# Expert weights read as one run per partition, with the tokens' features regrouped by a stride of 8

## The chip, the cores and the metric

The kernel runs on one core of a Trainium2 chip. The metric is the device time of one execution in microseconds (us). Less is better.

## What is computed

A network of three blocks on 512 tokens with 1024 features, in fp32. The change touches the first block's mixture of experts. Each token is sent to the best two of eight experts in the best of four groups (32 experts in all). Each expert has a gate and an up matrix of 1024 x 512 and a down matrix of 512 x 1024:

```python
def expert_block(args):
    xb, e = args
    a = xb @ w_e_gate[e]
    u = xb @ w_e_up[e]
    return (jax.nn.silu(a) * u) @ w_e_down[e]
...
y = jax.ops.segment_sum(y_rows * row_w[:, None], row_tok, num_segments=T)
```

The rows `xb` are tokens after an RMS norm whose gain vector `norm_ffn_g` has one factor per feature. Ahead of it come a gated convolution and a forgetting attention, behind it an mLSTM block with pooling and a latent attention block.

## The kernel before

The program is written engine by engine; semaphores order the engines against each other. Nothing schedules it: each engine's order is the order of the code.

**Dense products.** A weight matrix comes in slices of 256 columns, 1 MB each, through a ring of three buffers (`w_raw`). `load_slice(n)` on SP (L483 to L494) waits until the products of slice n - 3 are done and issues the load. ACT makes a high part of the slice (`w_hi`, L681), DVE the rest (`w_lo`, L1453), and PE multiplies in three passes (L1037 to L1039). Slices follow each other in the program's order: convolution (`cc`, `cu`, `cb`), `gconv`, `forget`, `conv_out`, then the attention's. ACT splits `conv_out`'s first slice after it has evicted the last `gconv` result.

**Experts.** Every expert gets a block of 64 token slots (`CAP`). Gate, up and down matrices have two buffers each, for even and odd experts. Experts 0 and 1 are loaded ahead (L497 to L499); the loop on SP (L524 to L532) loads expert e + 2's gate matrix when expert e's gate product is done, then up after the up product, and down after the down product. All three put 128 rows of the matrix on the 128 partitions: row `c * 128 + p` lies on partition p in chunk c, with 8 chunks for gate and up:

```python
gate_src = lambda e: t["w_e_gate"][bass.ds(e, 1)].rearrange("e (c p) n -> p (e c) n", p=P)
```

A partition thus reads 8 runs of 512 numbers (2 KB) for gate and for up, and 4 runs of 4 KB for down.

GpSimd gathers an expert's 64 rows of the normalised tokens from `h2_dram` into `xg` (64 partitions x 1024 features). On PE, `turn_rows` (L1205 to L1208) turns them so that features lie on the partitions: 8 transposes, each of which loads 128 columns of `xg` into the array and streams a 64 x 64 identity through it. DVE's `rows_in` (L1724) evicts the 8 results from PSUM to `xT` (128 x 8 x 64) and multiplies by the gain, of which `vec` holds feature `c * 128 + p` at partition p, column c. `xT` is the moving operand of the gate and up products, and its chunk c must hold the same features as chunk c of the matrix.

One expert on PE: gate product and up product, 64 matmuls each (fp32, 64 columns, L1215), then the turn of the **next** expert's rows, then the down product, 24 matmuls in three passes (L1037 to L1039). Beside it ACT and DVE split the down matrix (L681, L1741) and evict the results of the up product (L1748 to L1754).

```python
up_product(bank[2 + p], ring_gate[p], xT[p], gate_made)
...
up_product(bank[4 + p], ring_up[p], xT[p], up_made, bank[p], up_half)
...
turn_rows(1 - p, xt_turned)
```

The first turn stands ahead of the loop, so there are 33. Names used below: `xg` are the gathered rows, `xT` the turned ones, `down_hi` and `down_lo` the split down matrix, `hx` the product of silu(gate) and up, `gr` a small table loaded later in the program.

Of the kernel before, what the change touches and what calls it, by code (L numbers as in the profile page):

```python
# [16 lines left out]
F32 = mybir.dt.float32  # L17
# [7 lines left out]
P = 128  # L25
SEQ = 512
D = 1024
TT = SEQ // P
KC = D // P
# [8 lines left out]
CAP = 64  # L38
# [26 lines left out]
VECS = ["norm_mix_g", "conv_w0", "conv_w1", "conv_w2", "conv_b", "norm_ffn_g", "a_norm_g", "a_conv_w0",  # L65
        "a_conv_w1", "a_conv_w2", "a_conv_w3", "a_conv_b", "a_head_norm_g", "a_skip", "a_pool_scale", "c_norm_g"]
# [73 lines left out]
def build_kernel(nc, t):  # L140

    with ExitStack() as ctx:
        def at(name, shape, dt, offset):
            return nc.alloc_sbuf_tensor_at(name, shape, dt, offset=offset)
# [6 lines left out]
        def sem(name):  # L151
            if name not in sems:
                sems[name] = ctx.enter_context(nc.semaphore(name))
            return sems[name]


        bank = [ctx.enter_context(nc.psum_tensor(f"bank{i}", [P, 512], F32)) for i in range(8)]
# [6 lines left out]
        def misc(name, shape, dt):  # L164
            size = int(np.prod(shape[1:])) * (2 if dt == BF16 else 4)
            x = at(name, shape, dt, place[0])
            place[0] += -(-size // 32) * 32
            return x

        const = misc("const", [P, C_END], F32)  # L170
        vec = misc("vec", [P, V_END], F32)
# [22 lines left out]
        pos_i = misc("pos_i", [P, TT], I32)  # L194
        pos_f = misc("pos_f", [P, TT], F32)
        mark = misc("mark", [P, 8], F32)
        T0 = place[0]
        assert T0 + 12 * 2048 <= 229344, T0 + 12 * 2048

        def temp(name, i, shape=(P, 512), dt=F32, extra=0):  # L200
            return at(name, list(shape), dt, T0 + i * 2048 + extra)

        ident = const[:, C_ID:C_UP]
# [39 lines left out]
        xg = [at(f"xg{p}", [CAP, D], F32, BASE + 20480 + 4096 * p) for p in range(2)]  # L243
# [91 lines left out]
        x3_dram = nc.dram_tensor("x3_dram", (SEQ, D), F32).ap()  # L335
        h2_dram = nc.dram_tensor("h2_dram", (SEQ, D), F32).ap()
        y_dram = nc.dram_tensor("y_dram", (TOPK * SEQ + CAP, D), F32).ap()
        tok_view = lambda a: a.rearrange("(t p) d -> p t d", p=P)
        x_v = tok_view(t["x"])
        out_v = tok_view(t["out"])  # L340
# [3 lines left out]
        slice_no = {}  # L344
# [91 lines left out]
        def until_taken(eng, key):  # L436

            eng.wait_ge(drained[order[key] % 8], order[key] // 8 + 1)
# [45 lines left out]
        def _(sp):  # L484
# [13 lines left out]
                sp.dma_start(ring_up[p][:, :, :], up_src(e)).then_inc(up_landed[p], 16)  # L498
                sp.dma_start(ring_down[p][:, :, :], down_src(e)).then_inc(down_landed[p], 16)  # L499

            gate_src = lambda e: t["w_e_gate"][bass.ds(e, 1)].rearrange("e (c p) n -> p (e c) n", p=P)
            up_src = lambda e: t["w_e_up"][bass.ds(e, 1)].rearrange("e (c p) n -> p (e c) n", p=P)
            down_src = lambda e: t["w_e_down"][bass.ds(e, 1)].rearrange("e (c p) n -> p (e c) n", p=P)

            for tt in range(TT):
                sp.dma_start(x_tok[:, tt, :], x_v[:, tt, :]).then_inc(x_loaded[tt], 16)
            for n in range(slices1):
                if n == slice_no[("mix_out", 0)]:

                    until_taken(sp, ("OT1", KC - 1))  # L510
                    sp.dma_start(x1_tok[:, :, :], x_v).then_inc(x_back, 16)
                load_slice(n)
# [22 lines left out]
            with sp.If(count > 0):  # L535
                with sp.Fori(0, OVF) as i:
                    with sp.If(count > i):
                        sp.wait_ge(sem("ovf_free"), i + 1)
                        e = expert_of(i)
# [494 lines left out]
        def _(pe):  # L1034
# [156 lines left out]
            for b in range(TT):  # L1191
                ins = pe.matmul(out[:, TT * NE:(TT + 1) * NE], ones_b[:, :], hots[:, b, :, :].rearrange("p g e -> p (g e)"),
                                start=b == 0, stop=b == TT - 1)
# [4 lines left out]
            for q in range(TOPK * TT):  # L1198
                ins = pe.matmul(out[0:CAP, 0:NBLK], hot_slot[:, q, :], hot_block[:, q, :], start=q == 0, stop=q == TOPK * TT - 1)
# [4 lines left out]

            def turn_rows(p, done):  # L1205
                for j in range(KC):
                    ins = pe.transpose(bank[p][:, j * CAP:(j + 1) * CAP], xg[p][:, j * P:(j + 1) * P], ident[0:CAP, 0:CAP])
                ins.then_inc(done, 1)  # L1208

            def up_product(out, w, x, done, out2=None, half_done=None):  # L1210
# [19 lines left out]
            with pe.Fori(0, NE // 2) as i:  # L1230
                for p in range(2):
# [10 lines left out]
                    for f in range(FC):  # L1242
# [5 lines left out]
                        for a in range(2):  # L1248
                            half = slice(a * 512, (a + 1) * 512)
                            ins = parts3(bank[6 + a][:, :], hx_hi[p][:, f, :], hx_lo[p][:, f, :], down_hi[:, f, half],  # L1250
                                         down_lo[p][:, f, half], f == 0, f == FC - 1)
# [27 lines left out]
            for h in range(MH):  # L1279
                for tp in range(2):  # L1280
                    out = open_bank(pe, ("v2", h, tp))
                    for a in range(2):
                        tk = slice((2 * tp + a) * P, (2 * tp + a + 1) * P)
                        for c in (2 * h, 2 * h + 1):
                            ins = parts3(out[:, a * MD:(a + 1) * MD], xmT_hi[:, c, tk], xmT_lo[:, c, tk], wh[:, c, :], wl[:, c, :],
                                         c == 2 * h, c == 2 * h + 1)
# [3 lines left out]
            for name in ("q2", "k2"):  # L1290
                wh, wl = weights(slice_no[(name, 0)])
                for j in range(KC):
                    h, a = j // 2, j % 2
                    out = open_bank(pe, (name, j))
                    for c in (2 * h, 2 * h + 1):
                        ins = parts3(out[:, :], wh[:, c, a * P:(a + 1) * P], wl[:, c, a * P:(a + 1) * P], xcT_hi[:, c, :],
                                     xcT_lo[:, c, :], c == 2 * h, c == 2 * h + 1)
# [4 lines left out]
            for k, src in enumerate((g_i, g_e)):  # L1302
                for tt in range(TT):
                    ins = pe.transpose(out[:, (k * TT + tt) * MH:(k * TT + tt + 1) * MH], src[:, tt * P:(tt + 1) * P],
                                       ident[0:MH, 0:MH])
# [5 lines left out]
            for h in range(MH + 1):  # L1311
                if h < MH:
# [3 lines left out]
                    for sb in range(TT):  # L1316
                        out = open_bank(pe, ("ST", h, sb))
                        n = (TT - sb) * P
                        for c in (2 * h, 2 * h + 1):
                            ins = pe.matmul(out[:, 0:n], k2T[:, c, sb * P:(sb + 1) * P], q2T[:, c, sb * P:SEQ],  # L1320
                                            start=c == 2 * h, stop=c == 2 * h + 1)
                        ins.then_inc(results, 1)
                if h >= 1:
                    g = h - 1
                    for tt in range(TT):
# [5 lines left out]
                        for sb in range(tt + 1):  # L1331
# [3 lines left out]
                            ins = pe.matmul(out[:, MD:MD + 2], w, const[:, C_ONE:C_ONE + 2], start=False, stop=sb == tt,  # L1335
                                            skip_group_check=True)
# [12 lines left out]
            for j in range(KC):  # L1349
                g, a = j // 2, j % 2  # L1350
                out = open_bank(pe, ("pool", j))
                for c in (2 * g, 2 * g + 1):
                    ins = parts3(out[:, :], wh[:, c, a * P:(a + 1) * P], wl[:, c, a * P:(a + 1) * P], poolT_hi[:, c, :],
                                 poolT_lo[:, c, :], c == 2 * g, c == 2 * g + 1)
                ins.then_inc(results, 1)
            pe.wait_ge(sem("ya_lo_made"), KC)
            for c4 in range(4):
                banks = [open_bank(pe, ("w_out2", c4, tt)) for tt in range(TT)]
                for b, (xh, xl) in enumerate(((ya_hi, ya_lo), (yb_hi, yb_lo))):
# [3 lines left out]
                    for tt in range(TT):  # L1363
                        tk = slice(tt * P, (tt + 1) * P)
                        for c in range(KC):
                            ins = parts3(banks[tt][:, 0:256], xh[:, c, tk], xl[:, c, tk], wh[:, c, :], wl[:, c, :],
                                         b == 0 and c == 0, b == 1 and c == KC - 1)
# [30 lines left out]
            for s in range(4):  # L1398
                for name, c0, c1, n in (("uq", 0, nq, 2 * QKH), ("ukv", nq, 5, 512)):
                    wh, wl = weights(slice_no[(name, s)])  # L1400
                    for tt in range(TT):
                        out = open_bank(pe, (name, s, tt))
                        tk = slice(tt * P, (tt + 1) * P)
                        for c in range(c0, c1):
                            ins = parts3(out[:, 0:n], cT_hi[:, c, tk], cT_lo[:, c, tk], wh[:, c - c0, :], wl[:, c - c0, :],
                                         c == c0, c == c1 - 1)
# [31 lines left out]
        def _(dve):  # L1438
# [69 lines left out]
            for jj in range(4):  # L1508
                n = slice_no[("cc", jj)]
# [146 lines left out]
            for k, one in enumerate((one1, one2)):  # L1656
                ins = V.tensor_tensor(hot[:, k, :, :, :], one[:, :, :].unsqueeze(2).to_broadcast([P, TT, NG, EPG]),
                                      one_g[:, :, :].unsqueeze(3).to_broadcast([P, TT, NG, EPG]), ALU.mult)
# [59 lines left out]
            step(V.tensor_tensor(tok_w[:, 0, :], den, g_val, ALU.mult))  # L1718
            step(V.tensor_tensor(tok_w[:, 1, :], tok_w[:, 0, :], e2, ALU.mult))

            gain = vec[:, VECS.index("norm_ffn_g") * KC:(VECS.index("norm_ffn_g") + 1) * KC].unsqueeze(2).to_broadcast([P, KC, CAP])

            def rows_in(p, done):
                V.tensor_tensor(xT[p][:, :, :], bank[p][:, :].rearrange("p (c n) -> p c n", c=KC), gain, ALU.mult).then_inc(done, 1)  # L1724
# [11 lines left out]
            with dve.Fori(0, NE // 2) as i:  # L1736
                for p in range(2):
# [6 lines left out]
                    for half in range(2):  # L1744
                        n = FC // 2
# [46 lines left out]
            for s in range(4):  # L1792
                for j in (2 * s, 2 * s + 1):
# [8 lines left out]
                    for back in (1, 2, 3):  # L1802
                        ins = V.scalar_tensor_tensor(out=cv[:, back:], in0=src[:, 0:SEQ - back], scalar=vcol(f"a_conv_w{3 - back}", j),  # L1803
                                                     in1=cv[:, back:], op0=ALU.mult, op1=ALU.add)
# [34 lines left out]
            for h in range(MH + 1):  # L1839
                if h < MH:  # L1840
# [5 lines left out]
                    for sb in range(TT):  # L1846
# [5 lines left out]
                        n = (TT - sb) * P  # L1852
# [280 lines left out]
```

## Time and profile before

| | |
|---|---|
| runs shown | 2264.02, 2259.97, 2265.17 us |
| median | 2264.02 us |
| span of the profiled execution | 2262.5 us (its first to its last instruction) |
| PE busy | 2135.4 us, 94% of the span |
| DVE busy | 884.1 us, 39% |
| ACT busy | 709.5 us, 31% |
| moved by DMA | 335.00 MB, mean 148 GB/s |
| stage of the experts | about 791 to 1474 us of the span |

The profile is of one execution, and the page gives no time for it beside its span; what lies around the span, taken against the median, is 1.5 us. PE is TensorE's matmuls, PEld its loads of the stationary operand, DVE is VectorE, ACT ScalarE, POOL GpSimd, SP SyncE, which issues most DMAs. The granted clock (PEclk) is 1.00 at 2.4 GHz and 0.50 at 1.2 GHz. A line number such as L1207 is that of the kernel before.

### The profile page before, as it was taken

How to read it: one execution, taken by the hardware profiler on the slowest of the kernel's cores; microseconds unless marked ns; L12 is line 12 of the kernel's file. 1: busy time of each engine (PE TensorE's matmuls, PEld its weight loads, DVE VectorE, ACT ScalarE, POOL GpSimd, SP SyncE). 2: the span in 40 equal slices, each digit the busy share in tenths (PEclk: the TensorE clock that was granted, in tenths of full speed). 3: DMA queues.
4: the chain of work that ended last, by engine and by line, in shares of the span. 5: the costliest groups of instructions: out<-in, count | busy, mean ns of one | idle time of the engine just before them, and what ended most of it. 6: DMA issues, size and time to landing. Idle time of an engine off the chain costs nothing. (4 is left out here: it accounts for less than half of the span.)

```text
span 2262.5 us, 30876 instructions
## 1 busy us (share of the span) xinstructions
PE 2135.4 (94%) x12870; PEld 1862.6 (82%) x12870; DVE 884.1 (39%) x1476; ACT 709.5 (31%) x1010; POOL 103.3 (5%) x158
## 2 busy tenths in 40 slices
PE   7999999999999699999999999938999999998898
PEld 6888889766679599999999999836978889988568
DVE  4443221233344323323333333256343872335562
ACT  4222222322222303322332233243434222346431
POOL 0000000000000111110111011001000100000000
PEclk9999999755569779999999999969999999999899
DMA  6543555200015459999999999342312242222101
GB/s 140 94 98 98 96 96 96 68 1 0 1 50 190 173 181 335 334 330 330 332 334 328 331 332 334 130 181 84 94 38 75 75 132 94 71 76 69 47 1 56
DMA packets 189499, 335.00 MB, mean 148 GB/s; under 512 B 5088, under 2 KB 98016, under 8 KB 189408
## 3 DMA queue, kind: packets, MB, share of 16 engines
q1 hardware_dynamic: 183536, 315.32, 44.8%
q0 software_dynamic: 5440, 17.83, 2.1%
q8 instruction: 66, 1.08, 0.2%
q10 hardware_dynamic: 432, 0.56, 0.1%
q14 instruction: 25, 0.20, 0.0%
HBM read 318.49 MB, written 15.20 MB: 147 GB/s over the span
## 5 line engine op out<-in xcount | busy, mean ns | idle before, releaser
L1453 DVE TENSOR_TENSOR w_lo<-w_raw,w_hi 128x2048 fp32r<-128x2048 f32 (+2 forms) x97 | 211.6, 2183 | 474.8 <-ACT w_hi L681 474.6
L1741 DVE TENSOR_TENSOR down_lo<-down,down_hi 128x4096 fp32r<-128x4096 f32 x32 | 141.6, 4425 | 319.7 <-ACT down_hi L681 319.7
L681 ACT ACTIVATE w_hi<-w_raw 128x2048 fp32r<-128x2048 f32 (+2 forms) x97 | 176.8, 1823 | 266.5 <-PE bank L1039 114.8
L1215 PEld LDWEIGHTS bank<-xT,gate 128*128 128x128 f32 x2048 | 240.0, 196 | 3.5 <-issue 1.1
L1215 PE MATMUL bank<-xT,up 128*128 128x64 f32 x2048 | 240.5, 280 | 0.0
L1215 PE MATMUL bank<-xT,gate 128*128 128x64 f32 x2048 | 238.7, 279 | 0.9 <-DVE xT L1724 0.9
L1215 PEld LDWEIGHTS bank<-xT,up 128*128 128x128 f32 x2048 | 237.8, 196 | 0.0
L1037 PE MATMUL bank<-h1T_hi,w_hi 128*128 128x512 f32 x456 | 177.5, 389 | 0.6 <-DVE h1T_lo L1460 0.6
L1038 PE MATMUL bank<-h1T_lo,w_hi 128*128 128x512 f32 x456 | 177.4, 389 | 0.0
L1039 PE MATMUL bank<-h1T_hi,w_lo 128*128 128x512 f32 x456 | 177.4, 389 | 0.0
L681 ACT ACTIVATE ys<-bank 64x512 f32<-64x512 f32 x64 | 34.3, 584 | 425.2 <-PE bank L1039 425.2
L681 ACT ACTIVATE down_hi<-down 128x4096 fp32r<-128x4096 f32 x32 | 115.6, 3612 | 0.2
L1037 PE MATMUL bank<-h2T_hi,w_hi 128*128 128x512 f32 x264 | 103.6, 392 | 3.3 <-DVE hy_t L1890 2.2
L1037 PE MATMUL bank<-down_hi,hx_hi 128*128 128x512 f32 x256 | 104.3, 407 | 0.0
L1038 PE MATMUL bank<-h2T_lo,w_hi 128*128 128x512 f32 x264 | 103.4, 392 | 0.0
L1039 PE MATMUL bank<-h2T_hi,w_lo 128*128 128x512 f32 x264 | 103.4, 392 | 0.0
L1037 PEld LDWEIGHTS bank<-h1T_hi,w_hi 128*128 128x128 f32 x456 | 85.6, 188 | 18.6 <-issue 0.7
L1039 PE MATMUL bank<-down_hi,hx_lo 128*128 128x512 f32 x256 | 100.6, 393 | 0.0
L1038 PE MATMUL bank<-down_lo,hx_hi 128*128 128x512 f32 x256 | 100.2, 391 | 0.0
L1039 PEld LDWEIGHTS bank<-h1T_hi,w_lo 128*128 128x128 f32 x456 | 85.6, 188 | 17.7
L1038 PEld LDWEIGHTS bank<-h1T_lo,w_hi 128*128 128x128 f32 x456 | 85.6, 188 | 17.7
L1120 PE MATMUL bank<-v,pT_t 128*128 128x64 f32 (+1 forms) x480 | 98.8, 361 | 0.8 <-DVE pT_t L1585 0.8
(443 smaller groups left out, 4006.5 us busy)
## 6 DMA issues: line engine op xcount, KB each, us to landing
gate<-in_w_e_gate SPq DMA_DIRECT2D x32, 2048.0 KB, 9.9
up<-in_w_e_up SPq DMA_DIRECT2D x32, 2048.0 KB, 9.1
down<-in_w_e_down SPq DMA_DIRECT2D x32, 2048.0 KB, 10.1
w_raw<-in_w_in SPq DMA_DIRECT2D x32, 1024.0 KB, 9.6
w_raw<-in_a_w_in SPq DMA_DIRECT2D x20, 1024.0 KB, 5.2
w_raw<-in_a_w_out SPq DMA_DIRECT2D x8, 1024.0 KB, 5.3
w_raw<-in_c_w_in SPq DMA_DIRECT2D x6, 1024.0 KB, 5.3
w_raw<-in_w_conv_out SPq DMA_DIRECT2D x4, 1024.0 KB, 5.1
```

The costliest lines, as they stand in the source:

```text
L681: return nc.scalar.activation(out, in_, ACT.Copy, scale=scale)
L1037: pe.matmul(out, sh, mh, start=start, stop=False)
L1038: pe.matmul(out, sh, ml, start=False, stop=False)
L1039: return pe.matmul(out, sl, mh, start=False, stop=stop)
L1120: ins = pe.matmul(out[:, 0:width], pT_buf[k % 2][:, b, :], v_of(k, b), start=b == 0, stop=b == k % TT)
L1215: ins = pe.matmul(to[:, g * CAP:(g + 1) * CAP], w[:, c, f * P:(f + 1) * P], x[:, c, :], start=c == 0, stop=c == KC - 1)
L1453: V.tensor_tensor(ring_view(w_lo, n), ring_view(raw, n), ring_view(w_hi, n).bitcast(F32), ALU.subtract)\
L1741: V.tensor_tensor(down_lo[p][:, :, :], ring_down[p][:, :, :], down_hi[:, :, :].bitcast(F32), ALU.subtract)\
```

## The change

Gate and up matrices are put on the partitions in another order: row `p * 8 + c` lies on partition p in chunk c, so that the 8 rows of a partition are one run of 16 KB in DRAM. The down matrix keeps its order. `turn_rows` takes every eighth feature of `xg`, beginning at j, for its transpose j, so that `xT` has the same order as the matrices. The gain must be in that order too: a new tile `gain_pc` (128 x 8) replaces the slice of `vec`. It is made once: SP copies the 1024 gains from the input `vecs` to a DRAM tensor in the order of the features, in pieces of 4 bytes, waits for it, and loads them with 8 neighbours on each partition. DVE waits for this (`gain_loaded`) ahead of the loop.

```diff
+        gain_pc = misc("gain_pc", [P, KC], F32)
...
+        gain_dram = nc.dram_tensor("gain_dram", (D, 1), F32).ap()
...
-            gate_src = lambda e: t["w_e_gate"][bass.ds(e, 1)].rearrange("e (c p) n -> p (e c) n", p=P)
-            up_src = lambda e: t["w_e_up"][bass.ds(e, 1)].rearrange("e (c p) n -> p (e c) n", p=P)
+            gate_src = lambda e: t["w_e_gate"][bass.ds(e, 1)].rearrange("e (p c) n -> p (e c) n", p=P)
+            up_src = lambda e: t["w_e_up"][bass.ds(e, 1)].rearrange("e (p c) n -> p (e c) n", p=P)
...
             for n in range(slices1):
+                if n == slice_no[("conv_out", 0)]:
+                    g0 = VECS.index("norm_ffn_g") * KC
+                    sp.dma_start(gain_dram.rearrange("(c p) o -> p c o", p=P), t["vecs"][:, g0:g0 + KC].unsqueeze(2),
+                                 allow_slow_non_contiguous=True).then_inc(sem("gain_loaded"), 16)
+                    sp.wait_ge(sem("gain_loaded"), 16)
+                    sp.dma_start(gain_pc[:, :], gain_dram.rearrange("(p c) o -> p (c o)", p=P)).then_inc(sem("gain_loaded"), 16)
...
             def turn_rows(p, done):
                 for j in range(KC):
-                    ins = pe.transpose(bank[p][:, j * CAP:(j + 1) * CAP], xg[p][:, j * P:(j + 1) * P], ident[0:CAP, 0:CAP])
+                    rows = xg[p][:, :].rearrange("t (p c) -> t c p", c=KC)
+                    ins = pe.transpose(bank[p][:, j * CAP:(j + 1) * CAP], rows[:, j, :], ident[0:CAP, 0:CAP])
                 ins.then_inc(done, 1)
...
-            gain = vec[:, VECS.index("norm_ffn_g") * KC:(VECS.index("norm_ffn_g") + 1) * KC].unsqueeze(2).to_broadcast([P, KC, CAP])
+            gain = gain_pc[:, :].unsqueeze(2).to_broadcast([P, KC, CAP])
+            dve.wait_ge(sem("gain_loaded"), 32)
```

Two places show what this does to the order of instructions. The first is SP's queue at the end of the convolution, where `w_raw` is the ring of weight slices. Before:

```order
L494 DMA w_raw_49<-in_w_in 128x8x256 [waits results]
L494 DMA w_raw_50<-in_w_forget 128x1024 [waits results]
L494 DMA w_raw_51<-in_w_conv_out 128x8x256 [waits results]
L494 DMA w_raw_49<-in_w_conv_out 128x8x256 [waits results]
L494 DMA w_raw_50<-in_w_conv_out 128x8x256 [waits results]
```

With the change:

```order
L496 DMA w_raw_49<-in_w_in 128x8x256 [waits results]
L496 DMA w_raw_50<-in_w_forget 128x1024 [waits results]
L512 DMA gain_dram<-in_vecs 128x8x1
L515 DMA gain_pc<-gain_dram 128x8 [waits gain_loaded]
L496 DMA w_raw_51<-in_w_conv_out 128x8x256 [waits results]
```

The two small transfers, with the wait between them, stand ahead of the first load of `w_conv_out`; nothing else of the queue has moved.

The second is DVE ahead of the loop over the experts, from its last step of the routing to the first eviction of turned rows. Before:

```order
L1719 TENSOR_TENSOR tok_w<-tok_w,sm 128x4 [waits dve_step]
L1732 MEMSET hx_hi_135 128x512 [waits results,dve_step]
L1733 MEMSET hx_lo_137 128x512
L1732 MEMSET hx_hi_136 128x512 [waits dve_step]
L1733 MEMSET hx_lo_138 128x512
L1724 TENSOR_TENSOR xT_144<-bank,vec 128x512 [waits xt_turned,dve_step]
```

With the change:

```order
L1728 TENSOR_TENSOR tok_w<-tok_w,sm 128x4 [waits dve_step]
L1742 MEMSET hx_hi_136 128x512 [waits results,gain_loaded,dve_step]
L1743 MEMSET hx_lo_138 128x512
L1742 MEMSET hx_hi_137 128x512 [waits dve_step]
L1743 MEMSET hx_lo_139 128x512
L1734 TENSOR_TENSOR xT_145<-bank,gain_pc 128x512 [waits xt_turned,dve_step]
```

The first memset now waits for the gain as well, and the eviction reads `gain_pc`; the count and the order of the instructions are the same.

## Rows read from the trace of the kernel before

**Rows 1.** The page, part 1: busy us (share of the span) xinstructions.

```profile
PE 2135.4 (94%) x12870; PEld 1862.6 (82%) x12870; DVE 884.1 (39%) x1476; ACT 709.5 (31%) x1010; POOL 103.3 (5%) x158
```

**Rows 2.** Busy time by stretch: us, each engine's busy us, PEclk, DMA share, GB/s.

```profile
850.00:1440.00 590.00, 590.00 (x4609) 558.54 (x4609) 191.24 (x229) 183.81 (x146) 64.21 (x116) 1.00 0.96 329
```

**Rows 3.** Timeline of one expert: start us, us, engine, line [idle before].

```profile
1204.10 4.42 DVE L1741 TENSOR_TENSOR down_lo<-down,down_hi 128x4096 fp32r<-128x4096 f32 x1 [9.61 <-ACT down_hi L681]
...
1206.59 0.37 SPq L528 DMA_DIRECT2D gate<-in_w_e_gate  x1
...
1219.71 7.25 PE L1215 MATMUL bank<-xT,gate 128*128 128x64 f32 x64
1219.90 0.37 SPq L532 DMA_DIRECT2D down<-in_w_e_down  x1
...
1226.80 7.31 PE L1215 MATMUL bank<-xT,up 128*128 128x64 f32 x64
1227.14 0.37 SPq L528 DMA_DIRECT2D gate<-in_w_e_gate  x1
...
1234.04 0.71 PE L1207 MATMUL bank<-const,xg 64*128 64x64 f32 x8
```

**Rows 4.** The page, part 6: DMA issues of the experts, median us to landing.

```profile
gate<-in_w_e_gate SPq DMA_DIRECT2D x32, 2048.0 KB, 9.9
...
down<-in_w_e_down SPq DMA_DIRECT2D x32, 2048.0 KB, 10.1
```

**Rows 5.** Busy time by stretch while e1 is loaded ahead.

```profile
756.00:768.00 12.00, 12.00 (x92) 12.00 (x92) 0.00 (x0) 4.81 (x7) 1.49 (x2) 0.83 1.04 401
```

**Rows 6.** Waits of PE from 780 to 1470 us: us in total, times, longest.

```profile
PE bank L1207 <- DMA xg<-h_dram,get_row: 6.4, 1, 6.4
```

**Rows 7.** Busy time by stretch: the gate product beside loads and without.

```profile
1199.70:1206.20 6.50, 6.50 (x60) 6.50 (x60) 2.10 (x1) 4.30 (x3) 2.21 (x4) 1.00 0.97 337
1445.90:1452.40 6.50, 6.50 (x60) 6.46 (x59) 1.50 (x1) 4.58 (x3) 2.21 (x4) 1.00 0.21 45
```

**Rows 8.** L1207: the turn's loads (ns min/median/max), and timelines at both clocks.

```profile
L1207 PEld LDWEIGHTS bank<-const,xg x8: 178/221/221, 791.5 to 792.2; 64*128 64x128 f32 x8
...
L1207 PEld LDWEIGHTS bank<-const,xg x8: 134/138/142, 1213.5 to 1213.9; 64*128 64x128 f32 x8
...
821.01 0.93 PEld L1207 LDWEIGHTS bank<-const,xg 64*128 64x128 f32 x8
822.05 0.29 PEld L1037 LDWEIGHTS bank<-down_hi,hx_hi 128*128 128x128 f32 x1
...
1213.47 0.57 PEld L1207 LDWEIGHTS bank<-const,xg 64*128 64x128 f32 x8
...
1214.11 0.19 PEld L1037 LDWEIGHTS bank<-down_hi,hx_hi 128*128 128x128 f32 x1
```

**Rows 9.** Groups on DVE from 771 to 792 us: count | busy, mean ns.

```profile
L1674 DVE TENSOR_REDUCE counts<-hot_slot 128x8 f32<-128x256 f32 x1 | 0.4, 420 | 0.0
...
L1648 DVE TENSOR_REDUCE les<-wide 128x32 f32<-128x128 f32 x1 | 0.4, 375 | 0.0
...
L1649 DVE TENSOR_REDUCE sm<-les 128x4 f32<-128x32 f32 x1 | 0.2, 186 | 0.0
```

**Rows 10.** DMA issues with small pieces and of w_conv_out, median us to landing.

```profile
w_raw<-in_w_conv_out SPq DMA_DIRECT2D x4, 1024.0 KB, 5.1
...
gr<-in_c_kn_rope_g SPq DMA_DIRECT2D x1, 32.0 KB, 9.9
```

**Rows 11.** Timelines of SP and of ACT around the first load of w_conv_out.

```profile
177.30 0.34 SPq L494 DMA_DIRECT2D w_raw<-in_w_forget  x1
188.18 27.57 SPq L494 DMA_DIRECT2D w_raw<-in_w_conv_out  x4
...
199.56 1.91 ACT L681 ACTIVATE w_hi<-w_raw 128x2048 fp32r<-128x2048 f32 x1
```

**Rows 12.** Timeline before the first turn: the first gather.

```profile
787.52 0.96 POOL L596 DMA_INDIRECT xg<-h_dram,get_row  x1 [0.28 <-POOL get_row L604]
```

## The prediction

> **What bounds the kernel now.** I began with the page's shares: PE is busy for 2135.4 of 2262.5 us, 94% of the span [rows 1]. The change touches the stage with the experts, so next I asked for busy time by stretch. From 850 to 1440 us PE is busy for all of 590 us at a granted clock of 1.00, while the DMA share stands at 0.96 with 329 GB/s [rows 2]. Two resources look full at once; the two views after that tell which of them is the bound.
>
> First, the rhythm of one expert in order of time. The gate loads are issued at 1206.59 and 1227.14, so an expert takes 20.55 us, and PE goes from the gate product (1219.71, 7.25 us) to the up product (1226.80) to turning the next rows (1234.04) without a gap [rows 3]. A gate load is issued when the gate product of the expert two before it ends. It lands a median 9.9 us later [rows 4], and its matrix is wanted 34 us after the issue (two periods less the 7.25 us product): some 24 us to spare. The up load has as much. The down load is issued at 1219.90 and lands 10.1 us later, at 1230.0; its first reader, ScalarE's split, waits for the next down product's end, near 1240.5: 10 us to spare.
>
> Second, DMA has room. While expert 1 is loaded ahead, with nothing else in flight, the engines move 401 GB/s [rows 5], against 329 in the loop; the stretch holds pieces of 2 KB (gate, up) and of 4 KB (down). A DMA share near 1 at 329 GB/s is therefore overlapping transfers waiting on one another, not a queue that PE waits for. The list of PE's waits between 780 and 1470 us has one entry on a DMA, 6.4 us for the first gather, ahead of the loop [rows 6]. And loads do not slow PE down either: the same 6.5 us of the gate product hold 60 matmuls with DMA at 337 GB/s and 60 with 45 GB/s [rows 7]. **PE alone sets the 20.55 us.**
>
> **The change, part by part.**
>
> *Loads of 16 KB.* 64 transfers of 2 MB keep their bytes, but each partition now reads one run of 16 KB where it read eight of 2 KB. Whatever that saves lies in the 24 us to spare: 0. The cover is PE's 20.55 us per expert. It is gone only if PE needs less than DMA at its best: 6.3 MB at 400 GB/s are 15.7 us an expert; from there each per cent of rate would be worth 0.16 us an expert, 5 us in all. A worse rate would not be seen soon either: DMA can lose nearly a fifth (from 400 to 329 GB/s) before PE waits. The issue on SP stays one instruction per load. Gathers share the engines with longer pieces now, but one that is issued in an expert's gate product is read at the end of the next expert's up product, over 20 us on, so a few us of delay are free too: 0.
>
> *The turn with stride 8.* This is the part on the path. `turn_rows` runs once ahead of the loop and 32 times in it, 8 transposes each, 264 in all; [rows 8] has two of the turns. The rows xg are the operand that is loaded into the array; each load still takes 128 elements, but 32 bytes apart instead of side by side. Eight loads took 0.57 us with a median of 0.138 us for one, so one follows the other every (0.57 - 0.138) / 7 = 0.062 us; from the first load to the first load of the down product it is 1214.11 - 1213.47 = 0.64 us [rows 8]. Nothing hides more of it: the down product follows at once, whose low halves are made by 1208.5 (1204.10 + 4.42) [rows 3], and hx's second half is wanted only after 12 of its 24 matmuls. So every ns that a load takes longer is added 8 times per turn, 33 times.
>
> The trace of before has no strided load on PE. Bounds: at the low end 0, the load still pipelined at 0.062 us. Below nothing I exclude, since 128 elements must be read as before. At the high end the slowest stream of fp32 columns through PE in this stage: the gate product's 64 matmuls take 1226.80 - 1219.71 = 7.09 us, 0.111 us for 64 columns, which for 128 is 0.222 us: (0.222 - 0.062) x 8 x 33 = +42 us. Between them stand two near rows. One is the same turn where the granted clock was 0.50 (1.2 GHz, not 2.4): 822.05 - 821.01 = 1.04 us instead of 0.64 [rows 8], what it takes when columns come at half speed: +0.40 us. The other is a read with just this step of 32 bytes, on DVE: the sum over groups at L1648 reads 128 elements 8 apart in 0.375 us. Contiguous sums of 32 and 256 elements took 0.186 and 0.420 us [rows 9], so 1.04 ns per element, and 128 of them would cost 0.286 us. So the step made reading dearer by 0.089 us over 128 elements, 1.74 ns for one instead of 1.04: 1.7 times. It is the only row with this step, and it says that SBUF reads at 32 bytes come at something like half rate. I take half rate for PE too: +0.40 us a turn, 33 x 0.40 = **+13.2 us**.
>
> The Trainium skill, SBUF — State Buffer, in the note on cachelines under "Door 1: The DMA port swizzle", speaks against this change: lines of SBUF are 16 bytes, full bandwidth wants at least two hits in a line, and fp32 may stride by less than four elements for free. A step of 8 gives one hit per line; the page has no price, so by it the sum is more than 0 and no more can be said. The DVE row agrees, and no row here shows it for PE.
>
> *The gain.* `gain_pc` replaces a slice of `vec` in the multiplication that evicts xT (same shape, broadcast the same way): 0. Its making adds two DMAs on SP between the load of `w_forget` (177.30) and that of the first `w_conv_out` (188.18) [rows 11], and a wait for the first of them: 1024 pieces of 4 bytes from DRAM to DRAM. Behind the waiting SP stands the load of `w_conv_out`. SP is free for 10.5 us there anyway, since it waits for a result of PE. The nearest row is a load with pieces of 256 bytes, gr: 9.9 us with other loads about it [rows 10], so SP is back by 187.6, before 188.18. And were it 6 us later: the load takes 5.1 us [rows 10], landing at 193.3, and its split starts at 199.56 [rows 11]. 16 us in all, hence 0; beyond them each us late is a us of PE. The wait for `gain_loaded` on DVE comes 600 us later: 0.
>
> **Sum:** 0 + 13.2 + 0, on a profiled span of 2262.5 us: 2275.7. The median of the runs shown, 2264.02, has 1.5 us more around it than the span. Predicted 2277 us.
>
> **Rivals.**
>
> *A. The step costs PE nothing (0.32).* For it: PE reads through other hardware than DVE, and at a clock of 0.50 a load came every (0.93 - 0.221) / 7 = 0.101 us, at 1.00 every 0.062, not half of that [rows 8], so some of it is not column time and could hide a slower read. Against it: the part that is column time is the larger, and little would be hidden. Then nothing on the path changes: 2264. The Trainium skill, TensorE: Matmul & The Clock Gate, "LDWEIGHTS (loading the stationary operand)", has a load cost its columns divided by 1.2, in ns, and nothing else: 107 ns before and after. The trace has 62 ns from load to load, so the figure fails here, though its silence about strides may hold.
>
> *B. Each element costs PE a fetch of its own at the rate of the dear stream, 0.222 us a load (0.12).* For it: PE's loads run faster than one element per 0.5 ns, much faster than DVE's 1.04, so the fall could be steeper. Against: a ratio of 3.6, twice DVE's. +42 us: 2306.
>
> *C. SP comes back late (0.03).* It decides if the 4-byte pieces need more than 16 us to land; at 24 us PE stands 8 us: with the forecast's turn 2285. Against it: the small transfer of rows 10 needs 9.9 us.
>
> *D. The loads do bind, at the stage's start (0.05): faster.* Expert 1's load and the store of h2 lie right before the first gather, for which PE waits 6.4 us [rows 6]; with quicker loads the store and gather would come sooner. It decides only if the gather waits for engines. Against: it is issued at 787.52, after the table of rows is made [rows 12], when expert 1 has long landed. It needs rival A beside it; price: at most the whole wait: 2264 - 6.4 = 2257.6.
>
> That the pieces don't grow (16 KB cut again on the way) changes no term; it would show in the packet count alone.
>
> **How the numbers follow.** Forecast 0.48, A 0.32, B 0.12, C 0.03, D 0.05. About 0.2% (4.5 us) can be told from no change here. Faster is D, 0.05; same is A, 0.32; slower is the forecast, B and C, 0.63. The likeliest case's own range is a rate 1.45 to 2.2 times slower, 90 to 136 ns a load, +7.4 to +19.5 us: 2271 to 2284. The range must take in A with the scatter of the runs (2260 to 2265), and above a load of up to 150 ns (+23 us): 2260 to 2288. It leaves out B, and most of D and C.
>
> **What would show it.** Right: the eight loads of a turn take about 0.9 to 1.0 us instead of 0.57, the period grows from 20.55 to 20.95 us, gate and up products keep their 7.25 and 7.31 us, PE stays without idle time, and packets under 8 KB fall by some 65,000. The gate and up loads land earlier and nobody is earlier for it. Wrong: 0.57 us again (A), over 1.5 us (B), a hole in PE near 204 us (C), a shorter wait at 791 us (D); or a DMA-bound loop, seen as PE idle before L1215.

## The result and the profile after

The changed kernel takes 2274.57 us (median of 5 runs, 2270.27 to 2275.38), the kernel before 2264.67 us (5 runs, 2259.97 to 2265.9): 9.9 us more, a ratio of 1.0042 with a 95% interval of 1.003 to 1.0055. The profiled execution took 2274.69 us, 1.9 us of it around its span of 2272.8; its span is 10.3 us longer than that of before.

The page, the busy shares and the packets, beside [rows 1]:

```profile
PE 2145.7 (94%) x12870; PEld 1873.5 (82%) x12870; DVE 887.0 (39%) x1476; ACT 709.7 (31%) x1010; POOL 103.4 (5%) x158
...
DMA packets 133340, 335.01 MB, mean 147 GB/s; under 512 B 6273, under 2 KB 99201, under 8 KB 125057
```

PE has as many instructions as before and is busy 10.3 us longer: the whole loss is work of PE, not waiting. The pieces did grow: before, 189,408 of 189,499 packets were under 8 KB, now there are 64,351 fewer of these. Of 8 KB or more there were 91 and are now 8283, 8192 more: one for each of 128 partitions in 64 transfers, so the 16 KB went whole.

Where PE's time went is seen in one turn. Timeline of PE's loads (start us, us, engine, line, operation), one turn at a granted clock of 1.00, then one at 0.50, beside [rows 8]:

```profile
1220.01 0.96 PEld L1216 LDWEIGHTS bank<-const,xg 64*128 64x128 f32 x8
1221.03 0.19 PEld L1045 LDWEIGHTS bank<-down_hi,hx_hi 128*128 128x128 f32 x1
...
821.04 0.96 PEld L1216 LDWEIGHTS bank<-const,xg 64*128 64x128 f32 x8
822.12 0.28 PEld L1045 LDWEIGHTS bank<-down_hi,hx_hi 128*128 128x128 f32 x1
```

And all loads of the turn together (ns min/median/max, first and last start):

```profile
L1216 PEld LDWEIGHTS bank<-const,xg x264: 182/202/205, 791.5 to 1471.9; 64*128 64x128 f32 x132
```

Eight loads take 0.96 us instead of 0.57, and the down product starts 1.02 us after the first load instead of 0.64: +0.38 us for each turn at full clock. One load follows the other every (0.96 - 0.202) / 7 = 0.108 us, before every 0.062. At the half clock the 0.96 us are the same, where the contiguous turn took 0.93 [rows 8], and the down product comes after 1.08 us instead of 1.04. The stride costs 0.04 us there.

The loop over the experts, by its loads of the down matrix on SP (count, ns min/median/max, first and last start). First the kernel before, then the changed one:

```profile
L532 SPq DMA_DIRECT2D down<-in_w_e_down x30: 372/373/373, 829.1 to 1425.6; - x30
```

```profile
L540 SPq DMA_DIRECT2D down<-in_w_e_down x30: 383/383/390, 829.2 to 1436.1; - x30
```

That is 29 periods of 20.57 us before and of 20.93 after: +0.36 us each and +10.4 us together, about the whole difference of the spans (10.3). Two more turns come after the last of these loads. By the row above, the last load of a turn starts at 1471.9 us; before it was this:

```profile
L1207 PEld LDWEIGHTS bank<-const,xg x264: 134/139/221, 791.5 to 1460.7; 64*128 64x128 f32 x132
```

The stage begins at the same time in both. So the turns cost 11.2 us in all, 0.36 for each of the 31 at full clock, and the rest of the program took 0.9 us less, for which no run shows a reason.

Inside a period nothing else has changed. The up and gate products of the changed kernel, beside [rows 3]:

```profile
1212.77 7.31 PE L1224 MATMUL bank<-xT,up 128*128 128x64 f32 x64
...
1226.61 7.25 PE L1224 MATMUL bank<-xT,gate 128*128 128x64 f32 x64
```

Landings (median us, last column) beside [rows 4], the loop's busy time beside [rows 2], and the burst in which expert 1 is loaded ahead beside [rows 5]:

```profile
gate<-in_w_e_gate SPq DMA_DIRECT2D x32, 2048.0 KB, 8.8
up<-in_w_e_up SPq DMA_DIRECT2D x32, 2048.0 KB, 7.8
down<-in_w_e_down SPq DMA_DIRECT2D x32, 2048.0 KB, 8.5
```

```profile
756.00:768.00 12.00, 12.00 (x92) 12.00 (x92) 0.00 (x0) 4.81 (x7) 1.49 (x2) 0.83 0.96 392
850.00:1450.00 600.00, 600.00 (x4609) 569.25 (x4607) 193.68 (x228) 184.08 (x146) 64.32 (x116) 1.00 0.88 323
```

The gate loads land 1.1 us and the down loads 1.6 us earlier, the DMA engines are busy for 0.88 of the loop instead of 0.96, and PE is as full as before. Nobody waits for a load, so nobody is earlier. PE's waits from 780 to 1480 us are the same three as before, with the same 6.4 us for the first gather, beside [rows 6]:

```profile
PE bank L1216 <- DMA xg<-h_dram,get_row: 6.4, 1, 6.4
```

SP at the end of the convolution, beside [rows 11]:

```profile
177.28 0.34 SPq L496 DMA_DIRECT2D w_raw<-in_w_forget  x1
177.67 0.70 SPq L512 DMA_DIRECT2D gain_dram<-in_vecs  x1
187.15 0.35 SPq L515 DMA_DIRECT2D gain_pc<-gain_dram  x1
188.16 27.57 SPq L496 DMA_DIRECT2D w_raw<-in_w_conv_out  x4
```

The 4-byte pieces landed 9.5 us after their issue. SP was through with its next issue at 187.50, 0.7 us before PE's result let it go on, and the load of `w_conv_out` starts when it did before.

### The profile page after: what moved, and what is told of

Read it like the earlier page. It is cut to its first block and busy times, and to the rows that moved or that the text cites. A ratio compares the mean times of both kernels' runs of the same rounds, so it can differ in the third digit from the quotient of the medians.

```text
span 2272.8 us, 30878 instructions
## 1 busy us (share of the span) xinstructions
PE 2145.7 (94%) x12870; PEld 1873.5 (82%) x12870; DVE 887.0 (39%) x1476; ACT 709.7 (31%) x1010; POOL 103.4 (5%) x158
## 3 DMA queue, kind: packets, MB, share of 16 engines
q8 instruction: 66, 1.08, 0.2%
```

## The experiments

Two theories stood at the start. The first is the forecast's: only the turn costs, and 16 KB are worth nothing here. The rival is that 16 KB gain something and the turn costs more than the 10 us seen. Two kernels each make one half of the change.

**The turn alone.** The kernel before with only this:

```diff
-                    ins = pe.transpose(bank[p][:, j * CAP:(j + 1) * CAP], xg[p][:, j * P:(j + 1) * P], ident[0:CAP, 0:CAP])
+                    rows = xg[p][:, :].rearrange("t (p c) -> t c p", c=KC)
+                    ins = pe.transpose(bank[p][:, j * CAP:(j + 1) * CAP], rows[:, j, :], ident[0:CAP, 0:CAP])
```

> The kernel before with the turn alone changed: transposes read every eighth feature, the matrices stay in pieces of 2 KB and the gain is as before. (The rows then don't match the matrices, so the experts compute something else of the same size.) Theory, the turn's loads pay for the step: a load follows the other every 0.108 us instead of 0.062, the period is 20.92 us and the time is that of the changed kernel, about 10 us over before (2274 to 2276). Rival, the long pieces or the way to the gain slow the loop: the period stays 20.56 and the time that of before.

Measured: 2272.32 us against 2262.86 for the kernel before beside it, 1.0043 (1.003 to 1.0057). The loads have a median of 202 ns, the period is 20.92 us. The turn by itself makes the whole of the change's ratio.

**The loads alone.** The changed kernel, with the grouping by 8 moved from PE's reads to ScalarE's copy that makes the rows. They are stored in the new order, and the turn is contiguous again:

```diff
-                copy(h2_tok[:, tt, :], x1_tok[:, tt, :], rstd[:, tt:tt + 1]).then_inc(sem("h2_rows"), 1)
+                copy(h2_tok[:, tt, :].rearrange("t (c p) -> t p c", p=P), x1_tok[:, tt, :].rearrange("t (p c) -> t p c", c=KC),
+                     rstd[:, tt:tt + 1]).then_inc(sem("h2_rows"), 1)
...
-                    rows = xg[p][:, :].rearrange("t (p c) -> t c p", c=KC)
-                    ins = pe.transpose(bank[p][:, j * CAP:(j + 1) * CAP], rows[:, j, :], ident[0:CAP, 0:CAP])
+                    ins = pe.transpose(bank[p][:, j * CAP:(j + 1) * CAP], xg[p][:, j * P:(j + 1) * P], ident[0:CAP, 0:CAP])
```

> The changed kernel with 16 KB pieces and the reordered gain, but ScalarE writes the normalised rows into h2_tok already in the order p, c, so that the turn reads 128 neighbours as before. The result is the reference's. Theory: loads back at 0.062 us, period 20.56, time that of before within 2 us, since nothing waits for the matrices. If the long pieces had a gain of their own on the path, it would come out below before; if they had a cost, at 2266 or more. The four strided copies on ScalarE may take longer, but lie in 8 us of spare time.

Measured: 2264.37 us (11 runs) against 2262.86, 1.0004 (0.9995 to 1.0013). Loads of the turn, and PE's first wait in the stage (us in total, times, longest):

```profile
L1216 PEld LDWEIGHTS bank<-const,xg x264: 133/139/222, 792.6 to 1462.9; 64*128 64x128 f32 x132
```

```profile
PE bank L1208 <- DVE hot_block L1704: 6.8, 1, 6.8
```

The loads are back at 139 ns and the period at 20.57 us, with the landings of the changed kernel (8.8, 7.8, 8.5 us). So pieces of 16 KB are worth nothing in the period of this kernel. The stage begins 1.1 us later (792.6 against 791.5), with a wait of 6.8 us instead of 5.4 ahead of it; ScalarE's four copies that write the rows took 2.00 us each instead of 1.14. By the interval, from 1.1 us less to 2.9 us more than before, and with that late start, a gain or loss of some 2 us outside the loop is not excluded.

**Which steps cost?** By the 16-byte lines of the Trainium skill that the prediction cited (SBUF — State Buffer, the note on cachelines), a step of 8 bytes (two hits in a line) should cost less than 32 bytes. If distance counts, 16 bytes should cost less too. Both kernels keep the changed kernel's structure with smaller groups `c`. They also shorten the pieces, to 8 KB and 4 KB; between 16 and 2 KB the experiment above shows no difference beyond its interval. The main lines of the first edit:

```diff
-            gate_src = lambda e: t["w_e_gate"][bass.ds(e, 1)].rearrange("e (p c) n -> p (e c) n", p=P)
+            gate_src = lambda e: t["w_e_gate"][bass.ds(e, 1)].rearrange("e (b p c) n -> p (e b) (c n)", p=P, c=4)
...
-                    rows = xg[p][:, :].rearrange("t (p c) -> t c p", c=KC)
-                    ins = pe.transpose(bank[p][:, j * CAP:(j + 1) * CAP], rows[:, j, :], ident[0:CAP, 0:CAP])
+                    rows = xg[p][:, :].rearrange("t (b p c) -> t b c p", p=P, c=4)
+                    ins = pe.transpose(bank[p][:, j * CAP:(j + 1) * CAP], rows[:, j // 4, j % 4, :], ident[0:CAP, 0:CAP])
```

> As the changed kernel, but with a step of 4 features (16 bytes) and pieces of 8 KB. Theory, what counts is how many 16-byte lines of SBUF a load opens: with a step of 4 it still opens one for each element, so a load costs the same 0.108 us and the time is that of the changed kernel (+10 us). Rival, the price grows with the distance: about half, 0.085 us and +5 us.

> As the changed kernel, but with a step of 2 features (8 bytes) and pieces of 4 KB. Theory, lines: two elements per line, loads at 0.062 us, time that of before. Rival, any step breaks the fast path: 0.108 us and +10 us. Rival, distance: a quarter of the price, 0.074 us and +3 us.

Measured: 2276.4 us (1.0062, 1.0047 to 1.0078) with 16 bytes, 2280.45 us (1.0071, 1.0056 to 1.0087) with 8. A turn in each, 16 bytes first:

```profile
1219.31 1.03 PEld L1216 LDWEIGHTS bank<-const,xg 64*128 64x128 f32 x8
1220.41 0.19 PEld L1045 LDWEIGHTS bank<-down_hi,hx_hi 128*128 128x128 f32 x1
```

```profile
1202.19 1.03 PEld L1216 LDWEIGHTS bank<-const,xg 64*128 64x128 f32 x8
1203.29 0.19 PEld L1045 LDWEIGHTS bank<-down_hi,hx_hi 128*128 128x128 f32 x1
```

The eight loads take 1.03 us in both, slightly more than with 32 bytes, and a typical period is 21.00 us. Both theories fall, and the third of the last expectation, that any step pays, stands: the full price is paid at the smallest step that isn't 1, with two numbers in a line or with one. Why 8 and 16 bytes cost 0.07 us a turn more than 32 is open. The pattern differs in more than the step there: the slices begin in two or four blocks. At the half clock too the down product comes later with them, after 1.15 us, where it was 1.04 contiguous and 1.08 with 32 bytes.

The second kernel's profiled execution has something else besides. Two of its periods take 22.6 us; these stretches of it (length, busy us of PE, PEld, DVE, ACT, POOL, then granted clock, DMA share, GB/s) show why:

```profile
1040.00:1050.00 10.00, 10.00 (x92) 10.00 (x91) 4.42 (x1) 4.48 (x4) 2.21 (x4) 1.00 0.93 315
1050.00:1060.00 10.00, 10.00 (x57) 8.77 (x57) 2.30 (x7) 0.00 (x0) 0.00 (x0) 0.83 0.92 347
...
1260.00:1270.00 10.00, 10.00 (x65) 9.08 (x64) 2.56 (x8) 0.00 (x0) 0.00 (x0) 0.83 0.90 329
```

The 0.83 are the mean of 10 us. In slices of 1 us the clock is 1.00 up to 1054, 0.50 from 1055 to 1058 and 1.00 again from 1059, while PE was busy all the time: 2 x 1.6 = 3.2 us that belong to no step. Only this execution was profiled, but every run has a mean clock on record, and the time follows it: 2282.7 and 2281.87 us at 0.915 and 0.914, 2279.03 at 0.916, and 2276.14 at 0.918, which is the time of the kernel with 16 bytes (2276.4). The intervals of the two kernels overlap, so no price of 8 bytes over 16 is shown.

**What are 16 KB worth with less work on PE?** Two kernels, the one before and the changed one, with this in the gate and up products:

```diff
-                    for c in range(KC):
+                    for c in range(2):
                         ins = pe.matmul(to[:, g * CAP:(g + 1) * CAP], w[:, c, f * P:(f + 1) * P], x[:, c, :],
-                                        start=c == 0, stop=c == KC - 1)
+                                        start=c == 0, stop=c == 1)
```

> The kernel before with the gate and up products cut to 2 of 8 chunks (16 matmuls instead of 64 each; the sums over the other 6 chunks are left out), all loads kept. PE then needs 20.56 - 2 x 48 x 0.111 = 9.9 us per expert, and the loads should bind: 6.3 MB and 0.5 MB of rows at 401 GB/s are 17.0 us. It is the kernel that the next one is compared with.

> The changed kernel, cut in the same way, against the run before it. This shows what pieces of 16 KB are worth once nothing hides them. Theory, they raise the rate a little: the median landing in the loop fell from 9.9 to 8.8 us for gate and from 9.1 to 7.8 for up, so some 0.5 to 1.3 us per expert, 15 to 40 us in all. Rival, the engines are as fast with 2 KB: while expert 1 is loaded ahead, DMA moved 401 GB/s before and 392 after, so no difference.

Measured: 2186.41 us with 2 KB and 2186.55 with 16 KB. The same, but the pair doesn't answer the question. The periods are 18.70 and 18.69 us, not the 17.0 expected, and PE waits for the half of hx that comes last (2 KB, then 16 KB):

```profile
PE bank L1037 <- DVE hx_lo L1754: 206.2, 31, 7.4
```

```profile
PE bank L1045 <- DVE hx_lo L1764: 194.3, 31, 7.0
```

Behind that stands a chain: the down product frees the buffer, ScalarE and VectorE split, the next down product of 24 matmuls follows, at a granted clock of 0.77 in this loop. So I shortened this link too. In a second pair the down product is one pass:

```diff
-                            ins = parts3(bank[6 + a][:, :], hx_hi[p][:, f, :], hx_lo[p][:, f, :], down_hi[:, f, half],
-                                         down_lo[p][:, f, half], f == 0, f == FC - 1)
+                            ins = pe.matmul(bank[6 + a][:, :], hx_hi[p][:, f, :], down_hi[:, f, half], start=f == 0, stop=f == FC - 1)
```

> The kernel before with its loop over the experts made short enough for the loads to bind: the gate and up products add up only 2 of their 8 chunks, and the down product is one pass of 8 matmuls instead of three of 24 (the sums are not the experts' any more; every load, gather, split and turn is kept). What is left per expert beside the loads is ScalarE's split (3.6 us), VectorE's (4.4 us) and a down product of some 3 to 5 us, one after the other: 11 to 13 us. 6.3 MB of weights and 0.5 MB of rows at 400 GB/s are 16 to 17 us. I expect a period of 16 to 17 us, some 370 to 400 GB/s in the loop, the down load waiting on SP for less than before, and a time of about 2186 - 2 x 31 = 2125 us (2105 to 2150). If instead the period stays near 18.7 us, something other than loads or the down chain held the earlier pair.

> The changed kernel with the same cuts. Theory 1, pieces of 16 KB are worth nothing in rate: the burst ahead of the stage moved 401 GB/s with pieces of 2 KB and 392 with 16 KB, so the period is within 0.2 us of the other's, and the time within 6 us of it. Theory 2, they are worth what the DMA share shows, 0.88 instead of 0.96 in the loop for 323 against 329 GB/s, some 6% of the engines' time per byte: a period shorter by 0.6 to 1.0 us, and a time lower by 20 to 30 us. The landings, shorter by 1.1 to 1.6 us in the changed kernel's own loop, speak for theory 2; the burst speaks for theory 1.

Measured: 2154.99 us (2153.33 to 2157.36) with 2 KB, 2130.42 us (2127.75 to 2132.27) with 16 KB: 24.6 us or 1.1% less with 16 KB, so theory 2. With 2 KB the level is higher than the 2105 to 2150 us expected, since the loop moves less than 400 GB/s. Stretch 850 to 1250 and the down loads' issues with 2 KB, then the same with 16 KB:

```profile
850.00:1250.00 400.00, 200.09 (x1059) 178.87 (x1058) 142.10 (x176) 138.59 (x110) 48.70 (x88) 0.64 1.04 376
...
L532 SPq DMA_DIRECT2D down<-in_w_e_down x30: 372/6467/8686, 803.8 to 1324.4; - x30
```

```profile
850.00:1250.00 400.00, 195.41 (x1140) 174.33 (x1140) 148.57 (x184) 148.60 (x118) 53.12 (x96) 0.70 1.01 398
...
L540 SPq DMA_DIRECT2D down<-in_w_e_down x30: 383/384/390, 803.6 to 1294.7; - x30
```

That the loads bind now is seen on ScalarE. Its split of the down matrix waits for the down load, 104.4 us in all with 2 KB and 76.2 with 16 KB:

```profile
L681 ACT ACTIVATE down_hi<-down 128x4096 fp32r<-128x4096 f32 x32 | 115.7, 3616 | 104.4 <-DMA down<-in_w_e_down 104.4
```

```profile
L689 ACT ACTIVATE down_hi<-down 128x4096 fp32r<-128x4096 f32 x32 | 115.7, 3616 | 76.2 <-DMA down<-in_w_e_down 76.2
```

The periods are (1324.4 - 803.8) / 29 = 17.95 us and (1294.7 - 803.6) / 29 = 16.93 us, at 376 and 398 GB/s. Over the 29 periods that is 29.5 us; some 5 come back behind the loop, which I did not follow. With 2 KB something shows that a full DMA share does not: the issue of one load holds SP for several us. Timeline of SP there, 2 KB, then 16 KB:

```profile
1015.73 6.42 SPq L532 DMA_DIRECT2D down<-in_w_e_down  x1
1022.37 3.60 SPq L528 DMA_DIRECT2D gate<-in_w_e_gate  x1
1026.17 7.61 SPq L530 DMA_DIRECT2D up<-in_w_e_up  x1
1033.89 6.61 SPq L532 DMA_DIRECT2D down<-in_w_e_down  x1
```

```profile
1004.31 0.38 SPq L540 DMA_DIRECT2D down<-in_w_e_down  x1
1006.36 0.33 SPq L536 DMA_DIRECT2D gate<-in_w_e_gate  x1
1007.90 0.33 SPq L538 DMA_DIRECT2D up<-in_w_e_up  x1
1021.62 0.38 SPq L540 DMA_DIRECT2D down<-in_w_e_down  x1
```

With 2 KB, SP waits for PE in only 7.6 of the 400 us: nearly all its time goes into issues, I take it into a queue that has no room, which no row shows directly. With 16 KB the issues cost 0.33 to 0.38 us, and SP spends 300.0 of the 400 us waiting for the down product. What this pair doesn't separate is the engines' rate from the held SP; both go with the pieces.

The kernels of the change itself have this sign too, where expert 0 is loaded ahead of the stage. SP's issue of the down load, before the change and with it:

```profile
717.67 5.21 SPq L499 DMA_DIRECT2D down<-in_w_e_down  x1
```

```profile
716.80 0.49 SPq L501 DMA_DIRECT2D down<-in_w_e_down  x1
```

**How near was SP to being late?** The small transfer makes two more trips, each waited for, ahead of the load of `gain_pc`:

```diff
                     sp.wait_ge(sem("gain_loaded"), 16)
+                    for k in range(2):
+                        sp.dma_start(gain_dram.rearrange("(c p) o -> p c o", p=P), t["vecs"][:, g0:g0 + KC].unsqueeze(2),
+                                     allow_slow_non_contiguous=True).then_inc(sem("gain_again"), 16)
+                        sp.wait_ge(sem("gain_again"), 16 * (k + 1))
```

> The changed kernel with the 4-byte transfer and its wait done three times instead of once. Each took 9.5 us, so SP is back at about 206, 18 us late. The prediction gave 16 us in all before PE stands, of which one trip has used 9.5: 3 x 9.5 = 28.5 us are 12 us too many. Expected: a hole of about 12 us in PE before the first conv_out product (near 204), and 12 to 14 us more than the changed kernel, 2286 to 2289. Rival, later slices catch up: the hole is there but the time grows by less than half of it.

Measured: 2288.8 us (1.0109, 1.0093 to 1.0124), 14.2 us over the changed kernel. SP, and the wait of PE:

```profile
207.56 0.34 SPq L519 DMA_DIRECT2D gain_pc<-gain_dram  x1
207.95 2.46 SPq L496 DMA_DIRECT2D w_raw<-in_w_conv_out  x3
```

```profile
PE bank L1049 <- issue: 13.4, 1, 13.4
```

SP came back 207.95 - 188.16 = 19.8 us late and PE stood for 13.4: about 6 us are spare beyond SP's own wait, as the prediction had it. Later slices do not catch up: the whole hole is in the time. The three trips took 10.7, 8.1 and 11.3 us from issue to issue.

**The cold start of the stage.** At the half clock the stride of 32 bytes costs next to nothing, and the stage's first 30 us, two of its turns among them, run there. If PE does idle work (19 matmuls of 512 columns into a bank that nobody reads) in its waits ahead of the stage, does the clock stay up? The kernel before with:

```diff
+            def keep_warm(n):
+                for _ in range(n):
+                    pe.matmul(bank_of(("h2T", 5))[:, :], ident, const[:, 0:512], start=True, stop=True)
```

> The kernel before (2 KB pieces, turn of neighbours) with 19 idle fp32 matmuls of 512 columns on PE in the three waits for the routing between 771 and 791 us; their results are never read. The result is the reference's. Theory: expert 0 ran at a granted clock of 0.50 (gate product 13.91 us instead of 7.25, up 13.86 instead of 7.31, down 7.3 instead of 5.4) only because PE had stood idle; kept busy it starts at 1.00, and 13 to 15 us go: about 2249. Rival, the fp32 products of 64 columns pull the clock down by themselves and only the steady loop holds it: no gain, and what the idle matmuls run over is lost (0 to +5 us).

Measured: 2261.33 us against 2264.51, 0.9989 (0.998 to 0.9998). Stretches of it:

```profile
780.00:790.00 10.00, 9.81 (x37) 4.66 (x36) 7.89 (x33) 4.65 (x3) 2.60 (x4) 1.00 0.09 25
790.00:800.00 10.00, 8.93 (x55) 7.97 (x53) 6.13 (x5) 1.74 (x2) 4.85 (x2) 0.75 0.18 56
800.00:810.00 10.00, 10.00 (x48) 10.00 (x49) 0.00 (x0) 0.38 (x1) 0.00 (x0) 0.50 0.37 120
```

The clock was kept at 1.00 up to the gate product (from 780 to 790 us it is 0.50 in the kernel before), and fell to 0.50 all the same at 795 us, 2 us into that product, although PE was busy for 28.7 of the 30 us shown. The gate product takes 11.88 us instead of 13.91. So the idle time before the stage was not the only cause, and the theory fails; what pulls the clock down is not shown. Most of the hoped 13 to 15 us stay away; some 3 us, 0.1%, are left. Of the kernels that do all the work it is the only one that comes out under the kernel before, and barely.

## Why the prediction was right, and where not quite

- **PE alone sets the period.** Right. The gate product keeps its 7.25 us and the up product its 7.31, PE is busy for 600.00 of 600.00 us, and the loads' 1 to 1.6 us vanish in the spare time.
- **Loads of 16 KB: 0.** Right, shown by the kernel with the loads alone (1.0004). The margin was read too wide, though. The prediction took 6.3 MB at 400 GB/s, hence 15.7 us per expert, and let DMA lose nearly a fifth. It left out the rows that are gathered and stored: 376 GB/s for 17.95 us are 6.7 MB, which at 400 GB/s would be 16.9 us. In the loop where loads bind, 2 KB gave 376 GB/s and 17.95 us; that is an eighth under the 20.57 us of this kernel. And "each per cent of rate" was not empty: 16 KB give 5.9% of rate there, a period shorter by 1.02 us. The GB/s of the 12 us burst, 401 and 392 [rows 5], told nothing of it. The DMA share did, in the burst (1.04 to 0.96) as in the loop (0.96 to 0.88), and so did SP's issue of 5.21 us before the stage.
- **The turn: +0.40 us x 33 = +13.2 us.** The place, the sign and nearly the size are right: the turns cost 11.2 us, the medians differ by 9.9. The 2 us between 13.2 and 11.2 are two steps of the sum. Each of the 31 turns at full clock costs 0.36 us in the period, not 0.40 (1.2 us in all), and the price was put on the two turns at the half clock too, where the stride costs 0.04 us (0.7 us). Another 0.9 us are the rest of the program, and what is left lies between the spans profiled and the medians. That the price came so near is in part luck. The prediction speaks of half rate, but the +0.40 us were taken from the contiguous turn at the half clock, whose loads come every 0.101 us, 1.63 times 0.062; taken literally, twice 0.062 would have given +0.50. Measured are 0.108 us, 1.74 times, and DVE's ratio for this step was 1.7 [rows 9]. And a strided load comes every 0.108 us at either clock, so it is not the slower clock over again; what limits it is not shown.
- **Rival A (no cost)** is refuted by the 0.96 us. Its argument, that some of the 0.062 us isn't column time and could hide a slower read, fits the half clock only, where all but 0.04 us of a turn is hidden.
- **Rival B (0.222 us a load)** is refuted: 0.108.
- **Rival C (SP late)** did not happen. The load of 256-byte pieces was a good neighbour: 9.9 us for the 9.5 measured. It was no bound: the same transfer took 10.7 us in the kernel with three trips. SP was back 0.7 us before PE's next result, and with the 6 us behind it some 7 were left until PE would have stood; the experiment with three trips confirms these 6.
- **Rival D** did not happen: the wait of 6.4 us for the first gather is the same.
- **The Trainium skill, SBUF — State Buffer, the note on cachelines under "Door 1: The DMA port swizzle"**, warned against a step of 32 bytes, and the change is slower. Yet its lines do not explain why: by them fp32 with a step of 8 bytes is free, and it measured no less dear than 32. The page's figure of what is free is "4 fp32", which the prediction gave as less than four elements; four is the step of 16 bytes, and it cost the same 1.03 us. For PE's loads the traces tell side by side from not, and little more.
- **The Trainium skill, TensorE: Matmul & The Clock Gate, "LDWEIGHTS (loading the stationary operand)"**: 128 columns divided by 1.2 are 107 ns. The loads with a step of 32 bytes come every 108 ns, so it agrees with them; those of 8 and 16 bytes come every 116 and 117 ns ((1.03 - 0.220) / 7 and (1.03 - 0.213) / 7), and the contiguous ones every 62 ns at a granted clock of 1.00, where it does not.

## What to carry to other kernels

Regroup data on an engine that has time to spare (here ScalarE, once, for copies of 2.00 us instead of 1.14), and not in the operands that PE loads on the critical path: there each step tried, of 2, 4 and 8 numbers, raised a load from 0.062 to 0.108 us or more at full clock. Larger DMA pieces paid only in the kernels where loads bound. Look at the duration of the issues on SP and at the DMA share beside the GB/s, which can be equal where these two differ. Idle time of the engine that the loads feed tells whether any of it counts.

## What the runs showed of the hardware that was not expected

- A load of 128 columns with a step of 32 bytes follows the other every 0.108 us at a granted clock of 1.00 and of 0.50 alike (0.96 us for eight at 1220.01 and at 821.04). Contiguous ones change with the clock, 0.062 to 0.101 us.
- The size of the step hardly matters: 8, 16 and 32 bytes took 1.03, 1.03 and 0.96 us for eight loads, contiguous ones 0.57.
- An issue of a 2 MB load in pieces of 2 KB took SP 0.37 us in the loop of the kernel before. Where the loads bound, it took a median of 3.0 us for gate and 7.6 us for up, at most 11.3, and a median of 6.5 us for down with its pieces of 4 KB. In the kernel with pieces of 16 KB for gate and up it took 0.33 us (0.38 for down) at 398 GB/s.
- 1024 pieces of 4 bytes from DRAM to DRAM landed in 9.5 us, about as 32 KB in pieces of 256 bytes did [rows 10]; repeated, they took 8.1 to 11.3 us.
- The granted clock can fall while PE is busy all the time: from 1.00 to 0.50 at 1055 and at 1266 us in the kernel with steps of 8 bytes, and back within 4 us. And it fell from 1.00 to 0.50 in the first gate product of the kernel kept warm, after 20 us of almost unbroken work. What sets this off is open.
